# Two mixer layers in a new order: scores early, the other projections between the steps of the softmaxes, conditioning products beside the norm

## What is computed

```python
h = layernorm(x)
for layer in range(2):
    proj = h @ w_in[layer]                      # 1024 -> 4100 columns, split in 13
    (aq, ak, av, ag, bq, bk, bv, bf, bg, cq, ck, cv, cg) = split(proj)
    # a: 4 heads of 128, two softmaxes each, p1 - lam * p2, then a mean-square norm
    qa, ka = rope(aq), rope(ak)
    oa = rms(differential_attention(qa, ka, av, lam)) * silu(ag)
    # b: 4 heads of 64 with a cumulated forget gate in the logits
    cum = cumsum(log_sigmoid(bf + b_forget))
    ob = softmax(bq @ bk.T / 8 + cum[q] - cum[k]) @ bv * silu(bg)
    # c: 4 heads of 64, stick breaking: log_sigmoid of the scores, a reversed cumsum, exp
    oc = stick_breaking(cq, ck) @ cv * silu(cg)
    y = concat(oa, ob, oc) @ w_out[layer]
    h = layernorm(alpha * h + y)
mod = silu(c) @ w_ada                           # conditioning: 12 groups of 512 columns
```

## Time and profile before

| | us |
|---|---|
| time, median of 3 runs | 1880.21 (1879.91 to 1883.44) |
| the profiled execution's own time | 1882.82 |
| its span, first to last instruction | 1881.0 |
| TensorE busy in the span | 1648.2 (88%) |
| VectorE busy | 392.8 (21%) |
| ScalarE busy | 300.3 (16%) |
| first layer, first q product to the next layer's | 43.28 to 262.78 |
| second layer, first q product to the end of its variance | 262.78 to 471.25 |

### The profile page before, as it was taken

One profiled execution on the slowest core, in us unless ns is written; L12 is line 12 of the kernel. 1 busy time (PEld: TensorE's weight loads), 2 busy tenths in 40 slices (PEclk: granted clock), 3 DMA queues, 4 the chain that ended last, 5 costly groups with the idle time before them and its releaser, 6 DMA issues.

```text
span 1881.0 us, 19486 instructions
## 1 busy us (share of the span) xinstructions
PE 1648.2 (88%) x7938; PEld 969.1 (52%) x7938; DVE 392.8 (21%) x881; ACT 300.3 (16%) x587; POOL 2.8 (0%) x9
## 2 busy tenths in 40 slices
PE   3998799988799576869799999999999999999996
PEld 3786577857687465758633343333333333333342
DVE  2103411071101623721211111111111111111111
ACT  2013311151302401220200110110101001010010
POOL 0000000000000000000000000000000000000000
PEclk7998899999899777879799999999999999999998
DMA  7347534482233112203499999999999999999994
GB/s 251 133 125 227 187 106 155 143 313 74 79 114 134 45 45 90 90 31 149 148 402 427 428 429 429 428 429 428 428 429 429 429 428 429 428 428 429 429 428 202
DMA packets 86184, 515.04 MB, mean 274 GB/s; under 512 B 7000, under 2 KB 10776, under 8 KB 61560
## 3 DMA queue, kind: packets, MB, share of 16 engines
q1 hardware_dynamic: 82328, 513.43, 67.9%
q10 hardware_dynamic: 3632, 0.54, 0.2%
q0 software_dynamic: 176, 0.39, 0.1%
HBM read 511.20 MB, written 3.15 MB: 273 GB/s over the span
## 4 chain that ended last, share of the span: by engine, by line
PE 68%; DMA 17%; DVE 7%; ACT 4%; issue 2%; ACTq 1%; DVEq 0%; SPq 0%
PE psum L439 25%; PE psum L930 18%; DMA ring<-in_w_gu 15%; PE psum L999 8%; PE psum L903 3%; PE psum L448 3%; PE psum L479 2%; PE psum L913 2%; DMA ring<-in_w_ada 2%; PE psum L921 1%; DMA w_router<-in_w_router 1%; DVE sc L1405 1%; PE psum L496 1%; PE psum L815 1%; PE psum L480 1%
## 5 line engine op out<-in xcount | busy, mean ns | idle before, releaser
L930 PE MATMUL psum<-ring,hg 128*64 128x512 f32 x2048 | 458.6, 596 | 21.4 <-DMA ring<-in_w_gu 21.4
L439 PE MATMUL psum<-hT,ring 128*128 128x256 f32 x1504 | 342.4, 391 | 6.2 <-ACT hT L1190 6.2
L439 PEld LDWEIGHTS psum<-hT,ring 128*128 128x128 f32 x1504 | 296.0, 197 | 52.5 <-issue 9.9
L930 PEld LDWEIGHTS psum<-ring,hg 128*64 128x64 f32 x2048 | 139.2, 137 | 312.4 <-issue 267.7
L999 PE MATMUL psum<-w_down,hiddenT 128*64 128x512 f32 x1024 | 229.3, 600 | 28.2 <-ACT hiddenT L1365 25.2
L999 PEld LDWEIGHTS psum<-w_down,hiddenT 128*64 128x64 f32 x1024 | 74.9, 138 | 162.2 <-issue 162.2
L1767 DVE TENSOR_SCALAR gu<-psum 128x512 f32<-128x512 f32 x32 | 22.1, 692 | 529.2 <-PE psum L930 529.2
L1361 ACT ACTIVATE hidden<-gu 128x512 f32<-128x512 f32 x32 | 20.2, 630 | 316.2 <-DVE gu L1767 316.2
L439 PE MATMUL psum<-yT,ring 128*128 128x256 f32 x256 | 60.9, 403 | 9.3 <-DVE yT L1397 9.3
L903 PE MATMUL psum<-pick,h_tok 128*128 128x128 f32 x512 | 63.5, 284 | 2.9 <-DVE passes L1750 2.9
L903 PEld LDWEIGHTS psum<-pick,h_tok 128*128 128x128 f32 x512 | 60.5, 197 | 8.2 <-issue 8.2
(11 more groups left out here) (348 smaller groups left out, 1283.8 us busy)
## 6 DMA issues: line engine op xcount, KB each, us to landing
ring<-in_w_gu SPq DMA_DIRECT2D x128, 2048.0 KB, 22.5
w_down<-in_w_dn SPq DMA_DIRECT2D x64, 2048.0 KB, 20.7
ring<-in_w_in SPq DMA_DIRECT2D x24, 2048.0 KB, 8.0
ring<-in_w_ada SPq DMA_DIRECT2D x12, 2048.0 KB, 10.6
ring<-in_w_out SPq DMA_DIRECT2D x6, 2048.0 KB, 9.9
ring<-in_w_in SPq DMA_DIRECT2D x2, 2064.0 KB, 7.8
ring<-in_w_ssm_o SPq DMA_DIRECT2D x2, 2048.0 KB, 7.8
ring<-in_w_in SPq DMA_DIRECT2D x1, 2112.0 KB, 8.1
```

What stands on the lines that cost most here:

```text
L439: mm = pe.matmul(bank[0:m, c * T:(c + 1) * T], w[:, k, c0 + c * P:c0 + c * P + m], src[:, k, :], start=(k == 0), stop=(k == k_n - 1))
L930: mm = pe.matmul(psum[half * CAP:(half + 1) * CAP, 4 + part, :], hg[:, k, side, :], w[:, c0:c0 + 512], start=False, stop=(k == KC - 1), sk ...
```

## The change

The list of weight groups gets a new order: q, k, cqk, bqk, bvfg, ada, va, ada, cvg, ada, ga, the two of w_out, then three ada. TensorE's program follows it: rotations are made on both sides of the first cqk product, the scores of a on both sides of the bqk products, then the scores of c, and the remaining projections stand between the small products of the softmaxes and values. `ADA_AT` and `head_values`' calls go; `turn_head` and `head_value` are called one by one. Two of the six conditioning groups of a layer stand between the norm's mean and variance (`norm_sums(..., aside=2)`), one behind the variance. The gates are copied and `Silu` is applied later, all at once; `y_ready` comes in four steps, and the first w_out product takes its eight parts in the order 4 to 7, 0 to 3. ScalarE's and VectorE's programs are put in the order of TensorE's. No product and no element is added or left out, but for two one-element copies on VectorE.

```diff
-    FIRST_GROUPS = [("q", 0, 512), ("k", 512, 1024), ("va", 1024, 1536), ("ga", 1536, 2048),
-                    ("bqk", 2048, 2560), ("bvfg", 2560, 3076), ("cqk", 3076, 3588), ("cvg", 3588, 4100)]
+    FIRST_GROUPS = [("q", 0, 512), ("k", 512, 1024), ("cqk", 3076, 3588), ("bqk", 2048, 2560),
+                    ("bvfg", 2560, 3076), ("", 0, 1), ("va", 1024, 1536), ("", 0, 1), ("cvg", 3588, 4100),
+                    ("", 0, 1), ("ga", 1536, 2048)]
...
+        ada_groups(3)
...
-        def features(name, w, src, c0, n, m=P, ready=None):
+        def features(name, w, src, c0, n, m=P, ready=None, y_ready=None):
...
+            ks = range(k_n) if y_ready is None else (4, 5, 6, 7, 0, 1, 2, 3)
...
+                    if y_ready is not None and c == 0 and i % 2 == 0:
+                        pe.wait_ge(ev("y_ready"), 4 * y_ready + i // 2 + 1)
...
+            if aside:
+                ada(aside)
...
+        def turn_head(l, tag, h):
+            pe.wait_ge(ev("w" + tag), 4 * l + h + 1)
+            turn_rows(f"{l}.{tag}t{h}", sc[:, 2 * h, :] if tag == "a" else sf[:, h, :])
+
+        def head_value(l, tag, h):
+            name = f"{l}.oa{h // 2}" if tag == "a" else f"{l}.ob"
+            if name not in banks:
+                take(name)
+            read_out(pe, f"{l}.{tag}t{h}")
...
+            w = weights(f"cqk{l}")
             for j in range(2):
-                features(f"{L}ga{j}", w, hT, 256 * j, 2)
-            last_of(f"ga{l}", f"{L}ga1")
+                rotate(2 * j)
+                rotate(2 * j + 1)
+                features(f"{L}cqk{j}", w, hT, 256 * j, 2)
+            last_of(f"cqk{l}", f"{L}cqk1")
+
+            pe.wait_ge(ev("rope"), 4 * l + 4)
             w = weights(f"bqk{l}")
             for j in range(2):
+                for h in (2 * j, 2 * j + 1):
+                    for m in range(2):
+                        head_rows(f"{L}s{h}{m}", qk, h, qk, 4 + h, m)
                 features(f"{L}bqk{j}", w, hT, 256 * j, 2)
...
+            w = weights(f"bvfg{l}")
+            for b in range(NB):
+                tokens(f"{L}bv{b}", w, hT, b, 0, 256 + HB)
+            features(f"{L}gb", w, hT, 256 + HB, 2)
+            last_of(f"bvfg{l}", f"{L}gb")
+            ada(1)
+            w = weights(f"va{l}")
+            tokens(f"{L}va0", w, hT, 0, 0, 512)
 
             pe.wait_ge(ev("logf"), l + 1)
...
+            tokens(f"{L}va1", w, hT, 1, 0, 512)
+            last_of(f"va{l}", f"{L}va1")
             pe.wait_ge(ev("log_fail"), l + 1)
...
-            ada(3)
...
+            ada(1)
+            w = weights(f"cvg{l}")
+            tokens(f"{L}cv0", w, hT, 0, 0, 256)
+            for h in range(HB):
+                head_rows(f"{L}f{h}", bc_qk, h // 2, bc_qk, 2 + h // 2, h % 2)
+            turn_head(l, "a", 0)
+            turn_head(l, "a", 1)
+            tokens(f"{L}cv1", w, hT, 1, 0, 256)
+            read_out(pe, f"{L}va1")
+            head_value(l, "a", 0)
+            head_value(l, "a", 1)
+            turn_head(l, "a", 2)
+            turn_head(l, "a", 3)
+            features(f"{L}gc", w, hT, 256, 2)
+            last_of(f"cvg{l}", f"{L}gc")
+            head_value(l, "a", 2)
+            head_value(l, "a", 3)
+            turn_head(l, "f", 0)
+            turn_head(l, "f", 1)
+            ada(1)
+            w = weights(f"ga{l}")
+            features(f"{L}ga0", w, hT, 0, 2)
+            head_value(l, "f", 0)
+            head_value(l, "f", 1)
+            turn_head(l, "f", 2)
+            turn_head(l, "f", 3)
             o_bank = take(f"{L}oc")
...
-            pe.wait_ge(ev("y_ready"), l + 1)
+            head_value(l, "f", 2)
+            head_value(l, "f", 3)
+            features(f"{L}ga1", w, hT, 256, 2)
+            last_of(f"ga{l}", f"{L}ga1")
+
...
-            norm_sums(L, [f"{L}out{j}" for j in range(4)])
+            norm_sums(L, [f"{L}out{j}" for j in range(4)], aside=2)
+            ada(1)
...
+            for j in range(2):
+                read(f"{L}cqk{j}", bc_qk[:, 4 + 2 * j:6 + 2 * j, :])
+            exp_table()
             for j in range(2):
                 read(f"{L}bqk{j}", bc_qk[:, 2 * j:2 * j + 2, :])
+            for h in range(HC):
+                read(f"{L}z{h}", zs[:, h, :], cols=slice(0, W3), scale=HEAD ** -0.5)
+            act.wait_ge(ev("a_max"), l + 1)
+            row_exp(act, sc, 0, 8, row_max, row_sum, 0, 8, ev("a_exp"))
...
+            read(f"{L}gb", gate[:, 4:6, :])
+            f(ls[:, :, :], zs[:, :, :], ACT.Abs)
+            f(ls[:, :, :], ls[:, :, :], ACT.Exp, scale=-1.0)
+            f(ls[:, :, :], ls[:, :, :], ACT.Ln, ev("c_ln"), bias=1.0)
...
+            f(gate[:, 4:8, :], gate[:, 4:8, :], ACT.Silu, ev("gbc_silu"))
+            f(gate[:, 0:2, :], gate[:, 0:2, :], ACT.Silu, ev("ga_silu"))
+            read(f"{L}ga1", gate[:, 2:4, :], ACT.Silu)
...
+            weigh_a(0)
+            read_out(dve, f"{L}bv1")
+            tt(small[:, 0:8].rearrange("p (b h) -> p b h", b=NB), logf[:, :, :],
+               over(b_forget[:, l * HB:(l + 1) * HB], NB), ALU.add, ev("forget_x"))
+            weigh_a(1)
             dve.wait_ge(ev("c_ln"), l + 1)
             stt(flat(ls), flat(zs), 0.0, flat(ls), ALU.max, ALU.add)
             tt(ls[:, :, :], ls[:, :, :], over(K["strict_neg"][:, :], 4), ALU.mult, ev("log_fail"))
...
-            tt(yT[:, 0:4, :], yT[:, 0:4, :], gate[:, 0:4, :], ALU.mult, ev("y_ready"))
+            for j in range(2):
+                if j == 0:
+                    dve.wait_ge(ev("ga_silu"), l + 1)
+                else:
+                    read_out(dve, f"{L}ga1")
+                r = slice(2 * j, 2 * j + 2)
+                tt(yT[:, r, :], yT[:, r, :], gate[:, r, :], ALU.mult, ev("y_ready"))
```

More of the change, by code:

```diff
@@ L586, in _ @@
         ada.g = 0
+        def turn_head(l, tag, h):
[6 more added lines that the diff above has]
+            read_out(pe, f"{l}.{tag}t{h}")
+            bank, weight = psum[:, banks[name][0], :], probT[:, h % 2, :]
+            if tag == "a":
+                mm = apply_values(bank, h % 2, va, slice(h * P, (h + 1) * P), weight)
+                last = h % 2 == 1
+            else:
+                mm = apply_values(bank, h // 2, vbc, slice(h * HEAD, (h + 1) * HEAD), weight, h % 2)
+                last = h == HB - 1
+            if last:
+                full(mm, name)
+                b, n = banks[name]
+                values_done[(f"{l}.{tag}", h)] = (bank_full[b], n + 1)
+            else:
+                mm.then_inc(ev("values"), 1)
+                head_values.n += 1
+                values_done[(f"{l}.{tag}", h)] = (ev("values"), head_values.n)
         for l in range(DEPTH):
@@ L594, in _, with rotate @@
                 last_of(f"{name}{l}", f"{L}{name}1")
[L595 to L600, removed]
+            def rotate(j):
                 read_out(pe, f"{L}{'qk'[j // 2]}{j % 2}")
@@ L1251, in _ @@
+            turned("a", 2)
+            turned("a", 3)
+            read(f"{L}oa0", yT[:, 0:2, :])
+            read(f"{L}gc", gate[:, 6:8, :])
+            turned("f", 0)
+            turned("f", 1)
+            read(f"{L}oa1", yT[:, 2:4, :])
+            f(wide[:, 0:4, :], yT[:, 0:4, :], ACT.Square, ev("sq_a"))
+            read(f"{L}ga0", gate[:, 0:2, :])
+            turned("f", 2)
+            turned("f", 3)
             for j in range(2):
                 rstd(f"{L}ms{j}", wide[:, 4 + 2 * j:6 + 2 * j, :], 0, ev("rstd_a"))
+            f(gate[:, 4:8, :], gate[:, 4:8, :], ACT.Silu, ev("gbc_silu"))
@@ L1485, in _, with weigh_a @@
             maxima(sc, 8, row_max, 0, 8, ev("a_max"))
+            dve.wait_ge(ev("a_exp"), l + 1)
+            ch.after(dve.reciprocal(small[:, 16:32], row_sum[:, 0:16]))
+            ts(small[:, 32:48], small[:, 16:32], lam[:, 4 + l:5 + l], None, ALU.mult)
+            def weigh_a(h):
+                for cols, q in PARTS:
+                    r1, r2 = 16 + 8 * q + 2 * h, 32 + 8 * q + 2 * h + 1
+                    ts(sc[:, 2 * h + 1, cols], sc[:, 2 * h + 1, cols], small[:, r2:r2 + 1], None, ALU.mult)
+                    stt(sc[:, 2 * h, cols], sc[:, 2 * h, cols], small[:, r1:r1 + 1], sc[:, 2 * h + 1, cols],
+                        ALU.mult, ALU.add, ev("wa") if q else None)
+            weigh_a(0)
[3 more added lines that the diff above has]
+            weigh_a(1)
             dve.wait_ge(ev("c_ln"), l + 1)
@@ L1489, in _ @@
             tt(ls[:, :, :], ls[:, :, :], over(K["strict_neg"][:, :], 4), ALU.mult, ev("log_fail"))
+            dve.wait_ge(ev("forget_ln"), l + 1)
+            stt(logf[:, :, :].rearrange("p b h -> p (b h)"), small[:, 0:8], 0.0, small[:, 8:16],
+                ALU.min, ALU.subtract, ev("logf"))
+            weigh_a(2)
+            weigh_a(3)
             ch.free(dve.tensor_copy(cumq[:, :], product(dve, f"{L}cumq")[:, 0:NB * HB]), f"{L}cumq")
@@ L1501, in _ @@
             tt(sf[:, :, :], sf[:, :, :], over(K["row_mask"][:, :], HB), ALU.add)
+            for h in range(HC):
+                name = f"{L}after{h}"
```

(2 more changed lines are left out.)

121 lines of the change are left out of this document (28 added, 93 removed).

## The result

The changed kernel takes 1821.77 us (median of 4 runs, 1819.59 to 1825.07) against 1881.83 for the kernel before (4 runs, 1879.91 to 1884.57): a ratio of 0.968, 95% interval 0.966 to 0.970. The prediction was 1827.1 with a range of 1817 to 1841. The profiled execution took 1825.07 us, with a span of 1823.3; it is the slowest of the four.

A forecast was written before the change was run, and what follows sets the result against it. TensorE was taken to bound the layers, with waits paid twice through a slow clock. Savings of 28.1 and 25.0 us in the two layers sum to 53.1, giving 1827.1 us, range 1817 to 1841.

The forecast's parts named there:

- What bounds the kernel: In both layers TensorE sets the first and last stages, waits for others between, and restarts at 1.2 GHz after waits.
- The sum of the second layer: TensorE's work at full clock plus 0.5 us of wait: 186.5 us against 211.5 before, saving 25.0 us.
- The counted end: Second layer's lower bound, 185.7 us, with small products counted by columns; the upper end, from busy time, is 189.6.
- The walk: Second layer's new order followed event by event from the first q product: only `logf` late, by 0.5 us.
- tightest margin: Before w_out: last quarter of `y_ready` multiplied at 146.4, asked for at 147.5, 1.1 us to spare.
- The first layer: 186.5 plus 2.5 slow start plus 2.4 wait for va's weights behind the `bias_scratch` write: 191.4 us, saving 28.1.
- The sum: Both layers' savings, 25.0 and 28.1, make 53.1 us, for a predicted 1827.1 us.
- a warmer clock in the norms after the layers (-5): Allowance of 5 us in the range's lower end, for faster TensorE clock in the norms behind the two layers.
- the mixture: Rival, chance 0.14: TensorE's clock falls among the layers' mixed short products, turns and values, +9 us, giving 1836.
- exposed tail: Rival, chance 0.10: ScalarE is 2 us later, w_out waits again, 4.7 + 2.7 us a layer, giving 1842.
- lost at the experts: Rival, chance 0.03: expert loads are tied to a time of their own, so the gain vanishes, giving 1880.
- slower case: Rival, chance 0.04: `bias_scratch` write holds the queue 110 us, va comes 58 us later, giving 1885.

The follow-up runs named there:

- norm_part_alone: Kernel before with only the last three conditioning groups of each layer moved from before the turns into the norm (two before the variance, one behind): 1878.24 us.
- y_once: Changed kernel, but w_out waits for all four steps of `y_ready` before its first product, taking its parts in order 0 to 7: 1826.28 us.
- ga1_early: Changed kernel, but the second half of a's gate is projected ahead of the last turns, with `Silu` still at the end: 1835.19 us.
- shifted kernel: Kernel before with one idle VectorE operation of 1.8 us ahead of the gating of the first layer alone: 1877.99 us.
- norm_part_undone: Changed kernel with the norm's three conditioning groups put in a row between ga and w_out, the norm as in the kernel before: 1843.70 us.
- norm_part_spaced: Changed kernel, norm's three groups set apart (ahead of bvfg, between halves of va and of ga), `bias_scratch` write behind the fourth weight group: 1828.94 us.
- write_third: Changed kernel with the write of `bias_scratch` issued behind the third conditioning group instead of the first: 1837.66 us.

## Why the prediction was right, step by step

**What bounds the kernel.** The reading holds: what idle time was filled came off the time (33.5 us). The other 20.7 came as shorter busy time; the two w_outs (30.4 and 30.46 to 27.8) and the second q (29.55 to 28.16) have 6.7 of it by the clock, and the rest is not divided further. The runs with one part taken out or changed bear on the norm (8.3 us in the layers), the cover of the tail (14.0) and the steps of `y_ready` (3.4); no run took the early scores out alone, so for the waits for `sc` and for conditioning weights the evidence is the profile. Where a part was taken alone, in the stage where VectorE is late, it brought nothing, as norm_part_alone shows.

**The sum of the second layer.** 186.5 us were forecast between bounds of 185.7 and 189.6. Measured to the end of the variance it is 416.76 - 232.73 = 184.0, and 3.1 more by the count used there: 187.1. The counted end was the right one to be near; some small products came dearer: the scores of a and c, 2304 columns and 3.9 us by the prediction's count, took 4.8. With as much again from q's start and the eight products ahead of it, bvfg starts 64.4 us from the layer's start, where the walk's 76.5 for `gb` puts it at 62.6.

**The walk.** `logf` was forecast 0.5 us late and was 0.24. No bank and no other event held TensorE. The tightest margin was put at 1.1 us, for the last quarter of `y_ready`. VectorE's last multiplication of the gates ends at 379.95, and w_out, begun at 378.30, asks for it 2.6 us later, at 380.9: 0.9 us. y_once shows what it costs when the margin goes (3.4 us of waits), ga1_early when its cover goes.

**The first layer.** 191.4 was forecast, 189.7 measured (232.73 - 43.04). The arrival of va's weights was right: 52.5 us behind the write gave 126.5, and the product starts at 126.47. The mis-sized term is when TensorE wants them: 125.6, 1.5 us later than in the walk, so the wait is 0.85 and not 2.4 (1.28 in the second profile).

**The sum.** 53.1 us against 54.2 in the layers. The median fell by 60, and the 5 to 6 us between are in no term of the sum. 0.6 to 1.2 are in the norm after the layers. The rest lies from q2 on: 1384.9 and 1389.0 us in two profiles after, 1391.6 to 1392.3 in three before. The prediction had it only in the range, as "a warmer clock in the norms after the layers (-5)": the amount came, but the norms had 0.6 to 1.2 of it, and that the range's allowance fits is luck. The shifted kernel shows that the kernel before can lose 3 us by one more operation in the first layer. Why the clock falls where it does from q2 on, and whether the conditioning group behind the second variance helps the changed kernel there, stays open: norm_part_undone and y_once, one without and one with that group, have both falls, 1390.1 and 1390.8 us; norm_part_spaced, without it, has 1385.1.

**The rivals.** The clock does not fall in the mixture: 1.00 over 145.6 us in the second layer, with seven banks in turn. The many small gaps that the rival needed did not come: TensorE is idle for 0.24 us in that stretch. So what the Trainium skill tells in "TensorE: Matmul & The Clock Gate", section "A second HAM failure mode: psum-queue depth-cycling", of a clock that goes back and forth with short idles between groups is not tested by this kernel. Single waits ahead of w_out are: 1.5 to 1.8 us left it at 27.89, 2.8 to 3.8 gave 29.58, and 4.6 to 6.5 gave 29.5 to 30.5 over all the profiles. The exposed tail did not come, but ga1_early shows it at 13.4 to 14.8 us, at the 14.8 that it was priced at (4.7 + 2.7 a layer). Nothing was lost at the experts. The slower case needs a write that holds the queue for some 105 us; write_third has 55.8 as the worst.

## What to carry to other kernels

Work that is moved is worth its time only where its engine is what is late: taking three products away from before the turns gained nothing in the old order, and in the new one their place in the norms is worth some 8 us. Walk the new order event by event with durations from the trace, and put the walk's effort on the last producer before the next long stage, whose cover must be as long as the whole chain behind it. Count each short product's transfer too: three of 1.8 us in a row, 2 MB each, starved a ring of four slots.

## What was not expected of the hardware

- A kernel got 3.3 us faster (1877.99 against 1881.29) by one added VectorE operation of 1.8 us on its path. The clock falls at moments that hang on more than the length of the idle time before them: behind waits of 2.69 and 2.72 us the same product took 3.44 and 1.92 us in two profiles of the unchanged kernel. Differences of 3 to 5 us in this kernel should be read by stage before they are put down to an edit.

```profile
171.35 3.44 PE L581 MATMUL psum<-ring,condT 128*32 128x512 f32 x16 [2.69 <-DMA ring<-in_w_ada]
```

```profile
170.68 1.92 PE L581 MATMUL psum<-ring,condT 128*32 128x512 f32 x16 [2.72 <-DMA ring<-in_w_ada]
```

- A 2 MB write from eight partitions holds up what is issued behind it: weights landed 52.7 us after its issue with one group issued just ahead of it, and 55.8 with two, where the usual group takes 8. In the kernel before, 30 us after the write's issue, the DMA share is 0.45 at some 49 GB/s, though a conditioning group has been issued at 132.31:

```profile
149.00:153.00 4.00, 4.00 (x20) 3.54 (x19) 0.00 (x0) 0.38 (x1) 0.00 (x0) 1.00 0.45 49
```

0.45 of 16 engines are 7.2. The Trainium skill, "DMA: Bandwidth & Descriptors", section "Why a DMA increments its semaphore by 16 and not by 1", says that a transfer uses the largest number of engines, up to 16, that divides the slowest dimension of both its sides. That dimension is 8 here, and the trace fits eight engines that are busy nine tenths of the time. No run here tried another shape.
